# Memory keys and values of a hybrid decoder step: from a stage of their own to fp32 products behind the mixing steps

## The reference

```python
def memory_kv(mem, g_mem, w_xk, w_xv):
    mn = rmsnorm(mem, g_mem)                                   # (1, 256, 1024)
    k = (mn @ w_xk).reshape(B, N_MEM, X_HEADS, X_HD)
    v = (mn @ w_xv).reshape(B, N_MEM, X_HEADS, X_HD)
    return k, v

x = x + mixing(rmsnorm(x, g_mix), ...)      # one projection, three token mixers, w_out
x = x + cross_attn(rmsnorm(x, g_xattn), mem_k, mem_v, w_xq, w_xo)
x = x + swiglu(rmsnorm(x, g_ffn), w_gate, w_up, w_down)
```

## Time and profile before

| | |
|---|---|
| median of three runs | 2271.64 us (2265.46 to 2274.37) |
| profiled execution | 2273.51 us, span 2271.7 us |
| busy in the span | PE 90%, DVE 42%, POOL 32%, ACT 28% |
| mean granted clock of PE | 0.940 of 2.4 GHz |
| memory stage | layer 0: PE from 19 to 74 us; layer 1: 1126 to 1192 us |
| mixing steps of layer 0 | from 315 to about 467 us |

### The profile page before, as it was taken

One profiled execution on the slowest core, in us unless ns is written; L12 is line 12 of the kernel. 1 busy time (PEld: TensorE's weight loads), 2 busy tenths in 40 slices (PEclk: granted clock), 3 DMA queues, 4 the chain that ended last, 5 costly groups with the idle time before them and its releaser, 6 DMA issues. The chain is left out here.

```text
span 2271.7 us, 32497 instructions
## 1 busy us (share of the span) xinstructions
PE 2035.3 (90%) x14188; PEld 1909.5 (84%) x14188; DVE 945.1 (42%) x1319; ACT 631.7 (28%) x867; POOL 731.4 (32%) x358
## 2 busy tenths in 40 slices
PE   6999858689899999999899996676998999999995
PEld 5899747479789999999879995574995999999994
DVE  4543677533424330232173456774234243213313
ACT  4312542023323221222151126310323332222221
POOL 3333311323123334333343332122330333333331
PEclk9999967889999999999999997777999999999997
DMA  5432101252612222222243321012534122222221
GB/s 215 148 115 85 57 0 45 86 209 75 241 39 75 83 84 93 84 83 83 99 153 132 105 75 38 1 52 105 211 140 149 65 78 83 83 93 84 84 84 51
DMA packets 61238, 219.52 MB, mean 97 GB/s; under 512 B 10612, under 2 KB 11288, under 8 KB 58792
## 3 DMA queue, kind: packets, MB, share of 16 engines
q1 hardware_dynamic: 60216, 214.32, 27.1%
q10 hardware_dynamic: 880, 3.11, 0.4%
HBM read 202.47 MB, written 11.40 MB: 94 GB/s over the span
## 5 line engine op out<-in xcount | busy, mean ns | idle before, releaser
L945 POOL TENSOR_TENSOR WL<-RAW,WH 128x1024 fp32r<-128x1024 f32 (+1 forms) x276 | 646.3, 2342 | 1206.0 <-ACT WH L984 1206.0
L544 PE MATMUL PS<-XH,WH 128*128 128x288 f32 x2880 | 623.6, 298 | 17.4 <-DVE XL L1286 12.6
L544 PE MATMUL PS<-XH,WL 128*128 128x288 f32 x2880 | 619.2, 297 | 0.0
L544 PE MATMUL PS<-XL,WH 128*128 128x288 f32 x2880 | 619.0, 297 | 0.0
L984 ACT ACTIVATE WH<-RAW 128x1024 fp32r<-128x1024 f32 x276 | 292.6, 1060 | 1099.6 <-PE PS L544 1088.3
L544 PEld LDWEIGHTS PS<-XH,WH 128*128 128x128 f32 x2880 | 467.2, 190 | 22.9 <-issue 17.7
L544 PEld LDWEIGHTS PS<-XL,WH 128*128 128x128 f32 x2880 | 466.6, 190 | 0.0
L544 PEld LDWEIGHTS PS<-XH,WL 128*128 128x128 f32 x2880 | 466.6, 190 | 0.0
L544 PE MATMUL PS<-HH,WH 128*128 128x288 f32 x704 | 151.1, 296 | 3.6 <-DVE FT L1919 3.6
L544 PE MATMUL PS<-HH,WL 128*128 128x288 f32 x704 | 150.7, 296 | 0.0
L544 PE MATMUL PS<-HL,WH 128*128 128x288 f32 x704 | 150.6, 296 | 0.0
(11 more groups left out here) (261 smaller groups left out, 2496.3 us busy)
## 6 DMA issues: line engine op xcount, KB each, us to landing
RAW<-in_w_gu SPq DMA_DIRECT2D x88, 512.0 KB, 3.2
RAW<-in_w_dn SPq DMA_DIRECT2D x48, 512.0 KB, 3.2
RAW<-in_w_in SPq DMA_DIRECT2D x44, 512.0 KB, 3.3
KV<-in_cache_k SPq DMA_DIRECT2D x32, 512.0 KB, 7.4
KV<-in_cache_v SPq DMA_DIRECT2D x32, 512.0 KB, 5.8
RAW<-in_w_xk SPq DMA_DIRECT2D x16, 512.0 KB, 4.6
RAW<-in_w_xv SPq DMA_DIRECT2D x16, 512.0 KB, 3.2
RAW<-in_w_v SPq DMA_DIRECT2D x16, 512.0 KB, 3.2
```

Of the source, the lines that this page charges most:

```text
L544: return nc.tensor.matmul(out, lhsT=lhsT, rhs=rhs, start=start, stop=stop)
L945: nc.gpsimd.tensor_tensor(WL[:, s, w], RAW[:, r, w], WH[:, s, w].bitcast(f32), ALU.subtract).then_inc(split_done.sem, 1)
```

## The change

The stages "xk" and "xv" are gone; a layer starts with "in".

- **Memory products.** `mem` is normalised once per layer by DVE into `MN` (behind block 12 of "in"; the statistics are taken in layer 0 only, during blocks 4 to 9). The 16 weight units are loaded unsplit into six slots `MW` and multiplied in plain fp32. The slots lie in x's space and in `WH`/`WL`. PE does five key units ahead of the first step, the other three behind steps 1 to 3 and the eight value units behind steps 4 to 11, in banks 2 and 3. ACT copies them out.
- **Banks.** Prompt steps now use banks 0, 1, 4 and 6, 7, 5: outputs go to the second score bank, `back` to a first score bank. `scores(i)` so waits for the outputs of step i-2 to be taken and for a gate product, and `back` stands behind `keys`. DVE's gate product moves from the end of its iteration into `mask_scores`.
- **Residual in DRAM.** `MN`, `VOUT`, `KOUT` and two weight slots take x's space. x is written to the output `y` at the start of layer 1, and read back during the sample steps (in layer 0 from the input).
- **Start of a layer.** In layer 0 x comes in four parts ahead of all tables, and its split begins the kernel. In layer 1 the squares, `XH` and `XL` are formed during the last "dn" stage, and the two first splits of "in" too.
- **Moves.** DVE's halves of the weight rests are left in units 0 and 1 only. The first two "out" splits go from ahead of the steps to steps 12 to 14. The zeroing of `QE` goes from POOL to ACT, the decayed keys `KDG` from POOL to DVE. The bank of the third z product changes.

```diff
-STAGES = (("xk", 8, 8), ("xv", 8, 0), ("in", IN_BLOCKS, IN_BLOCKS), ("v", 8, 0), ("out", 8, 8),
+STAGES = (("in", IN_BLOCKS, IN_BLOCKS), ("v", 8, 0), ("out", 8, 8),
...
-SHARED = 18
+SHARED = 2
...
+        def output_bank(s):
+            return SCORE_BANK[s % 2] + 1 if STEPS[s][0] < NC else LAST_BANK[s % 2]
+        def back_bank(it):
+            return SCORE_BANK[(it - 1) % 2] if it <= 3 * NC else LAST_BANK[it % 2]
...
 (SyncE)
+                if l == 0:
+                    tokens_in(0)
+                    units("in", "w_in", 0, 1)
+                    for i in range(1, 4):
+                        tokens_in(i)
+                    units("in", "w_in", 1, 3)
...
+                else:
+                    units("in", "w_in", 0, 3)
+                    sp.wait_ge(gemm_evac.sem, gemm_evac.at(l, 0))
+                    sp.dma_start(o["y"], XT[:, :, :]).then_inc(x_spilled.sem, 16)
                 sp.dma_start(MRAW[:, :, :], t["mem"]).then_inc(mem_loaded.sem, 16)
...
+                sp.wait_ge(unit_done.sem, unit_done.at(l, U0["v"] + 8))
+                for n in range(2, 6):
+                    memory_unit(n)
+                memory_key_out(0)
+                memory_key_out(1)
+                for n in range(6, MEM_UNITS):
+                    sp.wait_ge(mem_used.sem, mem_used.at(l, n - 3))
+                    memory_unit(n)
+                    if n < 12:
+                        memory_key_out(n - 4)
...
+                sp.wait_ge(mv_out.sem, mv_out.at(l, 2))
+                sp.dma_start(o["mem_v"][l], VOUT[:, :, :]).then_inc(vout_stored.sem, 16)
+                for stored in kout_stored:
+                    sp.wait_ge(stored.sem, stored.at(l, 64))
+                sp.wait_ge(vout_stored.sem, vout_stored.at(l, 16))
+                sp.dma_start(XT[:, :, :], t["x"] if l == 0 else o["y"]).then_inc(xt_loaded.sem, 16)
...
 (TensorE)
+                def memory_keys(b):
+                    w = memory_weights(b)
+                    if b >= 2:
+                        pe.wait_ge(mk_out.sem, mk_out.at(l, b - 1))
+                    out = bank(LAST_BANK[b % 2], 0, NMEM)
+                    for k in range(KB):
+                        last = mm(out, w[:, 128 * k:128 * k + 128], MN[:, k, :], k == 0, k == KB - 1)
+                    last.then_inc(mem_used.sem, 1)
+                def memory_values(n):
...
+                    for a in range(2):
+                        k = 2 * (n % 4) + a
+                        for m in range(2):
+                            last = mm(bank(LAST_BANK[m]), MN[:, k, 128 * m:128 * m + 128], w[:, 512 * a:512 * a + 512],
+                                      k == 0, k == KB - 1)
+                    last.then_inc(mem_used.sem, 1)
+                pe.wait_ge(mn_ready.sem, mn_ready.at(l, 1))
+                pe.wait_ge(v_evac.sem, v_evac.at(l, 8))
+                for b in range(5):
+                    memory_keys(b)
                 pe.wait_ge(wi_used.sem, wi_used.at(l, 2))
...
                     if s >= 2:
                         if STEPS[s - 2][0] < NC:
-                            pe.wait_ge(sm_ready.sem, sm_ready.at(l, s - 1))
+                            pe.wait_ge(oc_ready.sem, oc_ready.at(l, s - 1))
...
+                    if s >= 4:
+                        pe.wait_ge(gated.sem, gated.at(l, s - 3))
...
                 for i in range(len(STEPS) + 3):
                     if i < len(STEPS):
                         scores(i)
+                        keys(i)
+                    if i == 3 * NC + 1:
+                        pe.wait_ge(mv_out.sem, mv_out.at(l, 2))
                     if 3 <= i:
                         back(i - 3, i)
-                    if i < len(STEPS):
-                        keys(i)
                     if 1 <= i <= len(STEPS):
                         outputs(i - 1)
+                    if 1 <= i < 4:
+                        memory_keys(4 + i)
+                    elif 4 <= i < 12:
+                        memory_values(i - 4)
...
 (ScalarE)
-                upper("v", 8)
-                upper("v", 9)
                 evacuate_v(1)
...
                 do(GA[:, :, :], GA[:, :, :], ACT.Ln, bias=1.0).then_inc(ga_ready.sem, 1)
+                memory_key_copy(0)
...
                 do(GA[:, :, :], GB[:, :, :], ACT.Exp, scale=1.0 / 16).then_inc(gexp_ready.sem, 1)
+                memory_key_copy(1)
...
                 for i in range(len(STEPS) + 1):
+                    if 2 <= i < 5:
+                        memory_key_copy(3 + i)
+                    elif i == 8 or i == 12:
+                        memory_value_copy(i // 4 - 2)
                     queries_apart(i + 1)
...
+                    if 3 * NC <= i < 3 * NC + SPLIT_SLOTS:
+                        upper("out", i - 3 * NC)
...
 (VectorE)
+                def normalise_memory():
...
+                    for k in range(KB):
+                        last = stt(MN[:, k, :], MRAW[:, k, :], gain("mem", k), RSM[:, :], ALU.mult, ALU.mult)
...
+                        if f == 1 and l + 1 < DEPTH and b % 2 == 1:
+                            for k in (b - 1, b):
+                                if b < KB - 1:
+                                    add_square(l + 1, sq_ready, sq_used, 0, k)
+                                x_rest(0, "mix", k, l + 1)
```

More of the change, by code:

```diff
@@ L41 @@
 PAIRS = 8
-Z_PAIRS = (3, 0, 1)
+Z_PAIRS = (3, 0, 2)
 EPS = 1e-6
@@ L149, in sb @@
             return place(name, shape, region(n), dt)
-        XT = sb("XT", [128, KB, NT])
+        r_x = region(4 * KB * NT)
+        XT = place("XT", [128, KB, NT], r_x)
+        MN = place("MN", [128, KB, NMEM], r_x)
+        VOUT = place("VOUT", [128, 2, D], r_x + 8192)
+        KOUT = place("KOUT", [128, 2, NMEM], r_x + 16384)
         r_xh, r_xl = region(4 * KB * NT), region(4 * KB * NT)
@@ L166, in build @@
         GT, V = place("GT", [128, PAIRS, NT], r_g), place("V", [128, NC + 1, VW], r_v)
[L167 to L172, removed]
+        MRAW = place("MRAW", [128, KB, NMEM], r_v)
+        MSQ = place("MSQ", [128, KB, NMEM], r_v + 8192)
         SBD = place("SBD", [128, 3, DEC_B, 128], r_v)
@@ L445, in _ @@
                 sp.dma_start(M0[:, :], t["m0"][l]).then_inc(lay_loaded.sem, 16)
[L446 to L453, removed]
+                units("in", "w_in", 3, 4)
                 units("in", "w_in", 4, 11)
@@ L531, in _ @@
                 for f in range(2):
-                    units(f"gu{f}", "w_gu", 0, 2 * FG, f)
+                    units(f"gu{f}", "w_gu", 0, 4, f)
+                    if f == 0 and l + 1 < DEPTH:
+                        sp.wait_ge(xl_ready.sem, xl_ready.at(l, 3 * KB))
+                        sp.dma_start(VECS[:, 0:NVEC], t["vecs"][l + 1]).then_inc(vecs_loaded.sem, 16)
+                    units(f"gu{f}", "w_gu", 4, 2 * FG, f)
                     units(f"dn{f}", "w_dn", 0, 12, f)
@@ L1063, in _ @@
                     upper("in", i)
+                    if l == 0 and i == 4:
+                        act.wait_ge(mem_loaded.sem, 16)
+                        do(MSQ[:, :, :], MRAW[:, :, :], ACT.Square).then_inc(msq_ready.sem, 1)
+                    elif l == 0 and i == 8:
+                        act.wait_ge(rsm_var.sem, 1)
+                        do(RSM[:, :], RSM[:, :], ACT.Sqrt).then_inc(rsm_sqrt.sem, 1)
                 for b in range(4):
@@ L1309, in next_norm @@
                     for b in range(KB):
+                        if n == 1 and b == 0:
+                            dve.wait_ge(xt_loaded.sem, xt_loaded.at(l, 16))
                         add_to_x(stage, b)
@@ L1781, in _ @@
                     if i < N:
-                        mask_scores(i)
+                        mask_scores(i, lambda: gate(i))
+                    else:
+                        gate(i)
+                    if i == 0:
+                        decayed_keys(CH, NT)
                     if N - 3 <= i - 0 < N:
```

436 lines of the change are left out of this document (245 added, 191 removed).

## The result

The changed kernel takes 2144.8 us, the median of four runs (2144.5 to 2145.7), against 2273.0 (2265.5 to 2278.8) for the kernel before beside it: a ratio of 0.944, with a 95% interval of 0.941 to 0.947. That is 128 us less, where 114 were forecast; 2144.8 lies inside the range and 13 us under the forecast of 2158.

What follows compares the result with a forecast made beforehand. TensorE was taken as the bound: at full clock in projections, with holes and a slow clock in the steps. -58.2 - 66.0 + 0.5 - 2.2 + 12 = -113.9 us from 2271.6 gave 2158 us, range 2138 to 2196.

Steps and rivals of the forecast that it cites:

- Start of layer 0: Head of layer 0: without the memory stage and with x in four parts, the third "in" block comes 58.2 us earlier.
- the marker: Point used to time a layer's head: the ten small products ending before the third "in" block, 89.4 and 1207.0 us before.
- Start of layer 1: Head of layer 1: squares and upper halves of x formed inside the last down projection; gain 66.0 us.
- Inside "in" and "v": These projection stages: memory statistics and normalising on DVE cost 0.5 us in all; 3 us if DVE fell behind.
- Ahead of the steps: Between "v" and first scores: ACT loses a 1.06 us split, 1.1 us a layer gained; five key units fit PE's hole.
- The steps: Prompt steps: memory units partly fill PE's waits at full clock; 5.9 us more a layer, 12 in all.
- Behind the steps: After the prompt steps: storing values and reading x back before the second state load costs 0, bound 3 us a layer.
- (a): Steps: memory units land on the path, not in holes; +38 us a layer, 2222 us, half of it 2190; chance 0.18.
- (b): Steps: PE's clock keeps alternating at a mean grant of 0.75; +31 us a layer, 2220 us; chance 0.09.
- (c): Steps and the hole before: clock stays at 1.2 GHz; +110 us a layer, 2378 us, slower than before; chance 0.02.
- (d): Steps: full clock shortens them, DVE sets the pace at some 7.8 us; -5 us a layer, 2136 us; chance 0.08.
- (e): Layer heads: x late or "in" starved, only half of the two 60 us gains comes; 2220 us; chance 0.03.

Runs made afterwards that it cites:

- experiment 10: The changed kernel with x of layer 0 loaded in one transfer in place of four, ahead of the first weight unit; 2149.8 us.
- Experiment 5: The kernel before, with only the multiply of the decayed keys moved from GpSimd to VectorE in two parts; 2269.0 us, ratio 0.997.
- experiment 6: The changed kernel with ScalarE's copies of the fourth and fifth memory key blocks put behind what the first scores need; 2145.0 us.
- experiment 1: The changed kernel with its eleven memory units inside the steps cut to one short product each, copies, loads and stores kept; 2136.9 us.
- experiment 2: The changed kernel with each of the eleven memory units inside the steps issuing its products twice; 2219.1 us, ratio 0.975.

## Why the prediction was right, and where it was off

- **Start of layer 0**, -58.2 forecast, -58.5 at the marker. First part of x at 5.4 us (5.3 forecast), "in" at 11.0 (9.5), third block at 30.9 (31.2). The chain is as forecast, and experiment 10 shows that it hangs on the first part; that the sum comes out within 0.3 us is in part luck. "in" began 1.5 us late and the statistics at 22.2 us for 20, but the second block took 6.7 us, 23.0 to 29.7, and not the 8.9 of the forecast. The 2.5 us for a low clock were laid on it, and the clock came up in the first block: its records stand 0.24 us apart until 15 us, 0.13 from there on.
- **Start of layer 1**, -66.0 forecast, -66.2. Right. The bound of 5 us for the late fourth unit wasn't needed.
- **Inside "in" and "v"**, +0.5 forecast, +0.4 in layer 0 between marker and end of "in", nothing in layer 1.
- **Ahead of the steps**, -1.1 a layer forecast, -3.1 and -2.9 measured. The step that failed is "ACT loses one 1.06 us split [...]: 1.1 us a layer", with the key decay's move to DVE costed as "both under the first products". That move wasn't free: it was the gain. Experiment 5 shows it alone, 3.6 us, because DVE's subtraction had been held beside GpSimd's multiply. The trace of before had the sign, 5.42 us for three operations whose like takes 1.9 later in the same trace; the forecast took the multiply's price and not what ran beside it. The Trainium skill, "SBUF — State Buffer", section "SBUF: two separate sides", says that a VectorE operation with two SBUF inputs and a GpSimd one that reads SBUF exclude each other for a whole instruction. The trace agrees: the first of the three subtractions starts at 306.03, just behind the multiply at 305.88, and ends at 310.25, when the multiply has been done since 309.70; the other two take 0.68 us each. Against that gain the changed kernel has its own delay: five units and a copy end later than the queries need, 1.7 us, which experiment 6 takes away. 3.6 less 1.7 is 1.9; the other 1.1 us of the 3.0 are as much as was forecast for ACT's split, which no run took apart.
- **The steps**, +5.9 a layer forecast; takes 4.1 us further apart and 1.7 to 1.8 less ahead of them: +2.4. The mechanism was right in the signs that it rests on: PE at a granted 1.00, no wait for a take, no wait for memory weights, no copy holding a product in these steps. PE's busy share came out at 95.0%, the edge of what was asked, and one sign ahead of the steps was wrong: the first scores waited for ACT, but ACT had waited for the fifth memory unit. Two figures of the working don't follow from the rows they name, and neither matters: six records in 1.53 us, the last of 0.38, stand 0.23 us apart on average and not 0.216 (a memory unit of the kernel after, 16 records from 261.10 to 264.72, does give 0.216), and DVE's 14.6 us in 20 are 18 in 25, not 19. The terms that were too large are PE's work, 93.2 us forecast (55.1 + 38.1) and 90.7 busy, and the pauses, 5.5 forecast and 4.8. Behind the one figure are two that the sum didn't part. With half units the stretch takes 87.1 us, 4.3 less than before in spite of the six banks, because the clock stays up; whole units then cost 8.5 us more. The hole in which half a unit is free is the wait for the shared bank: 11.9 us in experiment 1, 4.5 with half units, none with whole ones.
- **Behind the steps**, 0 forecast; -1.0 and -0.8 in the sample steps and -0.6 each in "out". They weren't traced to an instruction. In experiment 6 the sample steps take 1.5 us more, with a clock that falls earlier.
- **Sum.** -113.9 forecast, -128.4. Of the 14.5 us between them 3.8 lie ahead of the steps, 7.2 in them (the shorter way to the first take included), 3.0 behind them and 0.5 in the heads and "in". So 2144.8 lies in the range, but 11.0 us of the miss are in two terms: the stage ahead of the steps, where the key decay's move was taken for nothing, and the steps, whose price was too high.

**The rivals.** (a) is out: with the cover gone the eleven steps would have taken 38 us more, and they took 4.1 us more; PE waits for nothing in them. But its condition was close: experiment 2 is that rival, one unit further on. (b) and (c) are out: PE's grant is 1.00 in the eleven steps. The rule of the Trainium skill, "TensorE: Matmul & The Clock Gate", section "A second HAM failure mode: psum-queue depth-cycling", is that a kernel whose PE idles briefly between groups of matmuls oscillates between its two rates. Other traces of this case agree: it describes the kernel before (granted 0.80 in the steps) and experiment 1 (0.83), and the sample steps (0.74 in the changed kernel). It doesn't describe the changed kernel's prompt steps, as their pauses are filled. (d), DVE's pace at 7.8 us, is what half units come near to (7.9 us a step); whole ones put PE's work above it. (e) is out.

## What to carry to other kernels

Work that is moved into another stage's holes had two prices here: what overflows the holes, and what it does to TensorE's clock. To tell them apart, cut the work to half and double it, and read the granted clock beside the time. A step on the critical path whose row is longer than that of its like elsewhere in the trace may be held by a neighbour: see what GpSimd does in the same microseconds before costing the step's own work. And a gain ahead of a stage whose clock goes up and down can be lost in it, as in experiment 6.

## What was not expected of the hardware

- More work took less time: 2129.5 us with half units, 2136.9 with almost none. With almost none, PE's busy time over the steps is about the same (75.0 and 75.9 us), only at 0.83 for 0.97.
- The kernel before spreads by 24 us over its runs here, the changed one by 1.2 in four. Their clocks in the steps are 0.80 and 1.00 in the profiles; in the sample steps the clock falls in both.
- In "v" PE pauses for 2 and for 3 us in every kernel. "v" took 59.6 us in some profiled layers and 1.4 to 1.6 more in others, in which the clock fell behind the second pause (0.72 over six microseconds).
- Three subtractions of 512 columns took 1.9 us, and 5.4 beside one multiply on GpSimd.

What stays open: the 1 us in the sample steps and the 0.6 in "out", the share of the six banks as against the moved gate multiply, and how the sample steps, where PE is busy 36 of 58 us at a mean clock of 0.74, would do with more work in them. Of the kernels here that compute everything, the two with one unit in the first sample step were the fastest, 7 us under the changed one.
